# Tile starts at multiples of 128 bytes, the first weight tile loaded in halves, the result stored in runs, and one chunk's order, in a two-layer hybrid encoder trunk

## The chip, the cores and the metric

The kernel runs on one core of a Trainium2 chip. The metric is the device time of one execution in microseconds, lower is better. Before the change it is 2720.67 us (median of three runs).

## The reference, cut to what matters

The input is 512 positions of 1024 channels in float32. Two layers follow each other, each with a half-step feed-forward network, a mixer and a second half-step feed-forward network; a final RMSNorm ends it.

```
for l in range(2):
    x = x + 0.5 * swiglu(rmsnorm(x, ffn1_norm[l]), gate, up, down)        # 1024 -> 2816 -> 1024
    x = x + hybrid_mixer(rmsnorm(x, mix_norm[l]), w_in[l], ...)
    x = x + 0.5 * swiglu(rmsnorm(x, ffn2_norm[l]), gate, up, down)
return rmsnorm(x, final_norm)

def hybrid_mixer(h, ...):
    qkv, g_out, a, b, glu, gates = split(h @ w_in)
    q, k, v = silu(causal_depthwise_conv(qkv, 4 taps))                    # 8 heads of 128
    o = gated_delta_chunked(l2norm(q), l2norm(k), v, g, beta)             # chunked delta rule
    y_a = (rmsnorm(o, head_norm) * silu(g_out)) @ w_a_out
    c = val * sigmoid(gt)
    c = silu(rmsnorm(causal_depthwise_conv(c, 31 taps) + bias, conv_norm))
    y_b = c @ w_b_out
    return (sigmoid(gate_a) * y_a + sigmoid(gate_b) * y_b) @ w_o
```

## The kernel before, in words

**Products.** Everything is held transposed: channels on the 128 partitions, the 512 positions along the free axis. Each float32 operand is split into a high part (`_hi`, type float32r) and the rest (`_lo`), and a product is the sum of three TensorE matmuls, in the order w_hi x act_hi, w_hi x act_lo, w_lo x act_hi (`three`, line 441 on; every matmul is recorded at line 438). The activation is the moving operand and stands first in the names of a row (`h_hi,w_hi`). One output tile of 128 channels from 1024 channels is 8 k-steps of three matmuls, 24 matmuls with 512 columns; a tile of the down projection has 22 k-steps.

**Weights.** Weight tiles of 128x1024 go through four slots: SyncE issues the load into `raw`, ScalarE writes `w_hi` (`hi`, L855), VectorE writes `w_lo` (`lo`, L1235; in the heads a GpSimd DMA does it). TensorE waits for `lo_v`.

**Stages of a layer.** First network: a loop over 11 pairs of gate and up tiles with `h_hi`, `h_lo` as moving operand, then 8 down tiles with `act_hi`, `act_lo`. Mixer: the heads section multiplies `g_hi`, `g_lo` by the tiles of w_in (the first six tiles of a layer still use `h_hi`, `h_lo`), in pieces of 2 to 8 matmuls (mostly 6) between the small 128x128 matmuls of the previous head's delta rule (`PE_ORDER`); two of the gate tiles per chunk for the first three chunks are in it too. Then three tiles of w_a_out on `o_hi`, `o_lo`, three of w_b_out on `c_hi`, `c_lo`, a loop of five rounds with two gate tiles (g), one w_a_out tile (o) and one w_b_out tile (c), and 8 tiles of w_o on `mg_hi`, `mg_lo`. Then the second network. Of the 64 w_in tiles of a layer 6 read h, 48 read g in the heads section and 10 read g in the loop of five.

**Where the tiles lie.** `sb` puts each tile behind the last and rounds every size up to 64 bytes. The first tile, `cst`, lies at byte 16512, which is 129 times 128. The tiles up to `vs` have sizes that are multiples of 128 bytes. `pcol` has 8 x 49 x 4 = 1568 bytes, rounded to 1600, which is 12.5 times 128, so that `ssq`, `sqb`, `hf`, `YD`, `act_hi`, `act_lo`, `g_hi`, `g_lo`, `c_all`, `c_hi`, `mg`, `mg_hi` and `mg_lo` begin 64 bytes past a multiple of 128. `xT`, `h_hi`, `h_lo`, `raw`, `w_hi`, `w_lo`, and `o_hi`, `o_lo` (which share the place of h) begin at a multiple. `q_raw` with 2060 bytes, rounded to 2112, turns this round once more: from `qa` on (`cacc`, `kT`, `XT` and the rest of the delta rule, and `c_lo`) tiles begin at multiples of 128 again.

**The start.** SyncE issues x chunk 0, the first weight tile (512 KB), x chunks 1 to 7, then three more weight tiles. ScalarE issues the identity and then the parameters `pcol`, and multiplies x chunk 0 into `h_hi` when the parameters are there. The first two weight tiles are split by halves (`hi_halves`, `lo_halves`). TensorE runs ten matmuls on `ones` until then.

**The end of the mixer's convolution branch.** For each of 8 chunks VectorE does `c_norm` (L1738), `c_silu` (L1743) and `c_rest` (L1747, writes `c_lo`), ScalarE `c_tanh` (L1184) and the high part `c_hi` (L1191). After the last `c_hi` ScalarE goes on with `hi` of the next weight tiles, and VectorE with `lo`.

**The end.** The last down tile is computed in two halves of 256 positions. For each half: add, square, sum by TensorE, inverse root on GpSimd, spread by TensorE, then `last_norm` on VectorE multiplies in pieces of chunks, in place in `xT`, and SyncE stores each piece.

Of the kernel before, what the change touches and what calls it, by code (L numbers as in the profile page):

```python
# [17 lines left out]
P = 128  # L18
DEPTH, SEQ, D, FF, HEADS = 2, 512, 1024, 2816, 8
KT = D // P  # L20
# [4 lines left out]
EPS = 1e-6  # L25
SLOTS = 4
UNIT = KT * P
DSPLIT = [(0, 8), (8, 16), (16, 22)]
F32, F32R = mybir.dt.float32, mybir.dt.float32r
ACT = mybir.ActivationFunctionType  # L30
# [86 lines left out]
def trunk(nc, x, params_in, ffn1_w_gate, ffn1_w_up, ffn1_w_down, w_in, w_ab, a_log, dt_bias, head_norm, w_a_out, w_b_out, w_o,  # L117
          ffn2_w_gate, ffn2_w_up, ffn2_w_down, consts, out):
    ds = bass.ds
    with ExitStack() as ctx:  # L120
        place = [(nc.sbuf_base + 63) // 64 * 64]

        def sb(name, shape, dt=F32):
            t = nc.alloc_sbuf_tensor_at(name, [P, *shape], dt, offset=place[0])
            place[0] += (4 * int(np.prod(shape)) + 63) // 64 * 64
            return t


# [20 lines left out]
        hnh = sb("hnh", [1])  # L149
        hb = [*hf, *sqb]  # L150
        YD = sb("YD", [2 * P])
        arena = place[0]

        x_sq = sb("x_sq", [KT, SEQ])
# [7 lines left out]


        place[0] = h_at
        o_hi = sb("o_hi", [HEADS, SEQ], F32R)
        o_lo = sb("o_lo", [HEADS, SEQ], F32R)
        place[0] = arena
# [1 line left out]
        g_lo = sb("g_lo", [KT, SEQ], F32R)  # L169
        c_at = place[0]  # L170
        c_all = sb("c_all", [KT, SEQ])
        dn_at = place[0]
        q_raw = sb("q_raw", [SEQ + SC - 1])
        k_raw = sb("k_raw", [SEQ + SC - 1])
# [2 lines left out]
        assert place[0] - dn_at >= 2 * PRE * SEQ * 4  # L177
        c_raw = sb("c_raw", [SEQ + TAPS - 1])
        cacc = [sb(f"cacc{i}", [SEQ]) for i in range(2)]
        delta_at = place[0]  # L180
        (qT, kT, dec, thv, attn, qd, NT, X, XT, Y) = (
            sb(n, [SEQ]) for n in "qT kT dec thv attn qd NT X XT Y".split())
# [4 lines left out]
        hs = sb("hs", [HS_N, NC])  # L187
        sm = sb("sm", [7, NC])
        ksum = sb("ksum", [NC])
        ncol = sb("ncol", [PR_N])  # L190
        dcol = sb("dcol", [PR_N])
        dn_end = place[0]

        place[0] = c_at
# [25 lines left out]
        def sem(name):  # L220
            return ctx.enter_context(nc.semaphore(name))
# [2 lines left out]
        const_in = sem("const_in")  # L224
        ident_in = sem("ident_in")
        x_in = [sem(f"x_in{k}") for k in range(KT)]
        half_hi = sem("half_hi")
        half_lo = sem("half_lo")
        init = sem("init")
# [113 lines left out]
        def _(sp):  # L343
            def x_chunk(k):
                sp.dma_start(xT[:, k, :], x[k]).then_inc(x_in[k], 16)
# [15 lines left out]
            def ffn_units(l, w_gate, w_up, w_down, r_f, v_f, r_d, v_d):  # L361
                first = l == 0 and r_f == R_F1

                def pair_of(i):
                    for c in range(4):
                        src = tile((w_gate, w_up)[c % 2], l, i * 2 + c // 2)
                        unit(l * R_LAYER + i + r_f, l * V_LAYER + i + v_f, lo_v, c, src)
                        if first and isinstance(i, int) and c == 0:
                            for k in range(1, KT):
                                x_chunk(k)  # L370

                if first:
                    pair_of(0)
                with sp.Fori(int(first), FT // 2) as i:
                    pair_of(i)
                if first:
                    sp.dma_start(cst[:, 1:, :], consts[:, 1:, :]).then_inc(const_in, 16)
                if l < DEPTH - 1 and r_f == R_F2:
                    params(l + 1)
                with sp.Fori(0, 2) as i:  # L380
                    for c in range(12):
                        a, b = DSPLIT[c % 3]
                        src = tile(w_down, l, i * 4 + c // 3, a, b)
                        unit(l * R_LAYER + i * 3 + r_d, l * V_LAYER + i * 3 + v_d, lo_v, c, src, b - a)
# [7 lines left out]
            for l in range(DEPTH):  # L392
# [32 lines left out]
                    for c in range(4):  # L425
                        unit(l * R_LAYER + i + R_O, l * V_LAYER + i + V_O, lo_v, c, tile(w_o, l, i * 4 + c))
                ffn_units(l, ffn2_w_gate, ffn2_w_up, ffn2_w_down, R_F2, V_F2, R_D2, V_D2)
            stores = [(0, 0, 4), (0, 4, KT), (1, 0, 3), (1, 3, 6), (1, 6, KT)]
            for h, a, b in stores:
                sp.wait_ge(fin_y, h * KT + b)  # L430
                sp.dma_start(out[a:b].rearrange("k p s -> p k s")[:, :, side(h)], xT[:, a:b, side(h)]).then_inc(stored, 16)
            sp.wait_ge(stored, 16 * len(stores))


# [415 lines left out]
        def _(act):  # L850
# [29 lines left out]
            def ffn(l, w, r_f, r_d, nrm_i, upd0):  # L880
# [23 lines left out]
                for i in range(2):  # L904
                    for c in range(12):
# [22 lines left out]
                        if last and not end:  # L928
                            hi(l * R_LAYER + (r_d + 3 * i), c + 4)

            act.dma_start(cst[:, 0:1, :], consts[:, 0:1, :]).then_inc(ident_in, 16)
            act.dma_start(pcol[:, :, :], params_in[0]).then_inc(par_in, 16)

            def first_x(k):

# [5 lines left out]
                dst = ssq if m == 0 else x_sq[:, m, :]  # L941
                nc.scalar.activation(dst[:, :], xT[:, m, :], ACT.Square).then_inc(sq_done, 1)

            def hi_halves(c):

                act.wait_ge(raw_landed[c], 16)
                act.wait_ge(used, c + 1)
                nc.scalar.activation(w_hi[c][:, 0:UNIT // 2], raw[c][:, 0:UNIT // 2], ACT.Copy).then_inc(half_hi, 1)
                nc.scalar.activation(w_hi[c][:, UNIT // 2:], raw[c][:, UNIT // 2:], ACT.Copy).then_inc(hi_done, 1)

            act.wait_ge(init, 3)
            nc.scalar.activation(nrm[:, 2:4, :], pw[:, :, :], ACT.Copy, scale=pw[:, 1, 0:1])
            act.wait_ge(par_in, 16)
            first_x(0)
            hi_halves(0)
            for k in range(1, KT):
                first_x(k)
            hi_halves(1)
            for m in range(KT):
                square_first(m)  # L960
                if m in (2, 5):
# [267 lines left out]
        def _(dve):  # L1229
# [41 lines left out]
            def ffn(l, w, r_f, v_f, r_d, v_d, nrm_i, nf, row):  # L1271
# [58 lines left out]
                def last_norm(h, a, b):  # L1330

                    dve.wait_ge(fin_bc, h + 1)
                    dve.wait_ge(fin_w, KT - 1 + (h + 1 if b == KT else 0))
                    rs = bank[2 + h][:, side(h)].rearrange("p (k s) -> p k s", k=1).broadcast_to([P, b - a, HALF])
                    tt(xT[:, a:b, side(h)], xT[:, a:b, side(h)], rs, ALU.mult).then_inc(fin_y, b - a)

                for i in range(2):
                    for c in range(12):
                        if end and i == 1 and c == 11:
                            last_add(0)  # L1340
                            last_factor(0)
# [4 lines left out]
                            last_norm(1, 0, 3)  # L1346
# [20 lines left out]
                x_rest(k, PR_F1, 0)  # L1367

            dve.wait_ge(par_in, 16)
            def lo_halves(c):  # L1370

                dve.wait_ge(half_hi, c + 1)
                tt(w_lo[c][:, 0:UNIT // 2], raw[c][:, 0:UNIT // 2], w_hi[c][:, 0:UNIT // 2].bitcast(F32), ALU.subtract).then_inc(half_lo, 1)
                dve.wait_ge(hi_done, c + 1)
                tt(w_lo[c][:, UNIT // 2:], raw[c][:, UNIT // 2:], w_hi[c][:, UNIT // 2:].bitcast(F32), ALU.subtract).then_inc(lo_v, 1)

            first_rest(0)
            lo_halves(0)
            for k in range(1, KT):
                first_rest(k)  # L1380
            lo_halves(1)

            def sum_first(m):

# [9 lines left out]
            for l in range(DEPTH):  # L1394
# [24 lines left out]
                def columns(rd, hd):  # L1419

                    dve.wait_ge(ve_ds.sem, ve_ds.after(rd - 1, "v3"))
                    dve.wait_ge(ac_ds.sem, ac_ds.after(rd - 1, "v_tap"))
                    ts(dcol[:, :], pcol[:, hd, :], 1.0, None, ALU.mult).then_inc(*ve_ds.step("dcol"))
                    dve.wait_ge(ve_ds.sem, ve_ds.after(rd, "dcol"))

                def conv_tap(rd, t, j):
# [92 lines left out]
                def head(dense, hn, rn, before=True):  # L1519
# [41 lines left out]
                    def conv_input():  # L1561

                        if dn:
                            dve.wait_ge(taps, rn * CONV + CONV)
                            ts(ncol[:, :], pcol[:, hn, :], 1.0, None, ALU.mult)
# [196 lines left out]
                c_norm(1)  # L1762
                tail("vE", last)
                for k in range(KT):
                    c_silu(k)
                    if k + 2 < KT:
                        c_norm(k + 2)
                    c_rest(k)
                    if k == 1:
                        tail("oF", last)  # L1770
                        tail("ohi", last, 7)
                        tail("olo", last, 7)
# [189 lines left out]
```

## Time and profile before

| | us |
|---|---|
| runs (3) | 2720.61, 2720.67, 2720.92 |
| median | 2720.67 |
| the profiled execution's own time | 2720.52 |
| its span, first to last instruction | 2718.7 |
| TensorE busy | 2705.3, 100% of the span |
| VectorE busy | 1581.7, 58% |
| ScalarE busy | 1100.1, 40% |
| GpSimd busy | 258.2, 9% |
| mean granted TensorE clock | 0.999 |

Busy times are sums over the span; TensorE's matmuls overlap each other in the records (one is recorded with 390 ns while the next begins 227 ns later), so that the time per matmul is read from the distance of starts and not from the durations.

### The profile page before, as it was taken

What the parts mean: (1) busy time and instruction counts of PE and PEld (TensorE: products, weight loads), DVE (VectorE), ACT (ScalarE), POOL (GpSimd) and SP (SyncE); (2) the same over time, 40 slices, a digit from 0 to 9 for tenths busy, and PEclk for the clock granted to TensorE, in tenths of its full rate; (3) what the DMA queues carried; (4) which work ended last, traced back from release to release, by engine and by line L of the source; (5) the groups of instructions that cost most, each with busy time, mean ns of one, the idle gap of its engine ahead of it and who ended that gap; (6) DMA issues with size and microseconds to landing.
All of it is one profiled execution on the core that took longest, in us unless ns stands there. A gap on an engine that the chain in (4) does not pass through costs nothing.

```text
span 2718.7 us, 35832 instructions
## 1 busy us (share of the span) xinstructions
PE 2705.3 (100%) x13096; PEld 2251.9 (83%) x13096; DVE 1581.7 (58%) x2504; ACT 1100.1 (40%) x1849; POOL 258.2 (9%) x231
## 2 busy tenths in 40 slices
PE   9999999999999999999999999999999999999998
PEld 7888878888887888888888888788888878888887
DVE  6554357888885345553355543688888943455532
ACT  4222247766663232222222222566676622322222
POOL 0000022122120010000000000211212100100000
PEclk9999999999999999999999999999999999999999
DMA  4223335554542222233322233455556332222332
GB/s 166 96 97 104 92 101 140 130 142 111 136 126 93 98 88 100 93 101 93 102 93 93 100 93 96 108 131 140 125 124 145 96 108 93 93 100 93 97 94 66
DMA packets 84603, 292.04 MB, mean 107 GB/s; under 512 B 10001, under 2 KB 12689, under 8 KB 84497
## 3 DMA queue, kind: packets, MB, share of 16 engines
q1 hardware_dynamic: 69232, 235.85, 26.5%
q0 software_dynamic: 14976, 54.53, 10.9%
q8 instruction: 64, 1.05, 0.2%
q14 instruction: 43, 0.34, 0.0%
q10 hardware_dynamic: 288, 0.27, 0.0%
HBM read 233.99 MB, written 2.10 MB: 87 GB/s over the span
## 4 chain that ended last, share of the span: by engine, by line
PE 97%; DVE 2%; ACT 0%; issue 0%; DMA 0%; DVEq 0%; POOLq 0%; POOL 0%; ACTq 0%
PE bank L438 95%; PE bank L637 1%; PE bank L689 1%; DVE c_lo L1747 0%; DVE w_lo L1235 0%; ACT c_hi L1191 0%; PE bank L651 0%; PE bank L725 0%; DVE sqb L1743 0%; DVE hf L1743 0%; DMA pcol<-in_params_in 0%; DVE hf L1738 0%; PE bank L458 0%; DVE NT L1664 0%; ACT w_hi L855 0%
## 5 line engine op out<-in xcount | busy, mean ns | idle before, releaser
L1235 DVE TENSOR_TENSOR w_lo<-raw,w_hi 128x1024 fp32r<-128x1024 f32 x342 | 422.6, 1237 | 542.2 <-ACT w_hi L855 542.1
L855 ACT ACTIVATE w_hi<-raw 128x1024 fp32r<-128x1024 f32 x446 | 469.8, 1055 | 658.7 <-PE bank L438 658.6
L438 PE MATMUL bank<-h_hi,w_hi 128*128 128x512 f32 x1504 | 587.1, 390 | 2.2 <-DVE h_lo L1260 2.1
L438 PE MATMUL bank<-h_hi,w_lo 128*128 128x512 f32 x1504 | 585.5, 389 | 0.0
L438 PE MATMUL bank<-h_lo,w_hi 128*128 128x512 f32 x1504 | 585.3, 389 | 0.0
L438 PE MATMUL bank<-g_hi,w_hi 128*128 128x512 f32 x928 | 384.2, 414 | 0.0
L438 PE MATMUL bank<-g_hi,w_lo 128*128 128x512 f32 x928 | 378.7, 408 | 0.0
L438 PE MATMUL bank<-g_lo,w_hi 128*128 128x512 f32 x928 | 369.6, 398 | 0.0
L438 PEld LDWEIGHTS bank<-h_hi,w_hi 128*128 128x128 f32 x1504 | 282.3, 188 | 63.3 <-issue 3.6
L438 PEld LDWEIGHTS bank<-h_hi,w_lo 128*128 128x128 f32 x1504 | 282.3, 188 | 58.8
L1535 DVE SCALAR_TENSOR_TENSOR cacc<-c_raw,ncol,cacc 128x512 f32<-128x512 f32 x464 | 330.0, 744 | 0.4
L438 PEld LDWEIGHTS bank<-h_lo,w_hi 128*128 128x128 f32 x1504 | 282.4, 188 | 57.7
L438 PE MATMUL bank<-act_hi,w_hi 128*128 128x512 f32 (+1 forms) x726 | 281.3, 387 | 0.0
L438 PE MATMUL bank<-act_hi,w_lo 128*128 128x512 f32 (+1 forms) x726 | 279.6, 385 | 0.0
L438 PE MATMUL bank<-act_lo,w_hi 128*128 128x512 f32 (+1 forms) x726 | 277.0, 382 | 0.0
L890 ACT ACTIVATE hf<-hf 128x512 f32<-128x512 f32 x88 | 55.6, 632 | 447.3 <-DVE hf L1282 447.3
L1845 POOL TENSOR_TENSOR ssq<-ssq,sqb 128x512 f32<-128x512 f32 x41 | 54.8, 1337 | 1708.0 <-ACT sqb L869 1708.0
L438 PEld LDWEIGHTS bank<-g_hi,w_lo 128*128 128x128 f32 x928 | 175.0, 189 | 31.3
L438 PEld LDWEIGHTS bank<-g_lo,w_hi 128*128 128x128 f32 x928 | 175.5, 189 | 28.2
L438 PEld LDWEIGHTS bank<-g_hi,w_hi 128*128 128x128 f32 x928 | 175.9, 190 | 22.9
L438 PEld LDWEIGHTS bank<-act_hi,w_lo 128*128 128x128 f32 x726 | 136.2, 188 | 30.0
L438 PEld LDWEIGHTS bank<-act_lo,w_hi 128*128 128x128 f32 x726 | 136.3, 188 | 28.7
(258 smaller groups left out, 3355.5 us busy)
## 6 DMA issues: line engine op xcount, KB each, us to landing
raw<-in_w_in SPq DMA_DIRECT2D x128, 512.0 KB, 3.3
w_lo<-raw POOLq DMA_DIRECT2D x104, 512.0 KB, 4.6
raw<-in_ffn_w_gate SPq DMA_DIRECT2D x88, 512.0 KB, 3.2
raw<-in_ffn_w_up SPq DMA_DIRECT2D x88, 512.0 KB, 3.2
raw<-in_ffn_w_down SPq DMA_DIRECT2D x64, 512.0 KB, 3.5
raw<-in_ffn_w_down SPq DMA_DIRECT2D x32, 384.0 KB, 3.1
raw<-in_w_a_out SPq DMA_DIRECT2D x16, 512.0 KB, 3.2
raw<-in_w_b_out SPq DMA_DIRECT2D x16, 512.0 KB, 3.2
```

What stands on the lines that cost most here:

```text
L438: return nc.tensor.matmul(o, a, b, start=start, stop=stop, **kw)
L637: m = nc.tensor.transpose(o[:, c * P:c * P + P], a[:, c * P:c * P + P], ident)
L689: m = nc.tensor.transpose(bank[2][:, q * P:q * P + P], X[:, q * P:q * P + P], ident)
L855: nc.scalar.activation(w_hi[c % SLOTS][:, :], raw[c % SLOTS][:, :], ACT.Copy).then_inc(hi_done, 1)
L890: nc.scalar.activation(sg_f[f][:, :], sg_f[f][:, :], ACT.Silu).then_inc(silu_done, 1)
L1235: tt(w_lo[c % SLOTS][:, :], raw[c % SLOTS][:, :], w_hi[c % SLOTS][:, :].bitcast(F32), ALU.subtract).then_inc(lo_v, 1)
L1535: stt(out=acc[:, :], in0=src, scalar=ncol[:, j:j + 1], in1=acc[:, :], op0=ALU.mult, op1=ALU.add).then_inc(taps, 1)
L1845: tt(ssq[:, :], ssq[:, :], sqb[m % 2][:, :], ALU.add).then_inc(sums, 1)
```

## The change

`sb` rounds the place up to a multiple of `LINE` = 128 before a tile of 512 bytes or more, and so do the bases `arena`, `dn_at` and `delta_at`. In the built program every tile of at least 512 bytes then begins at a multiple of 128; those that began at one before keep that property (some move by 256 bytes). The order of tiles is the same.

At the start the first weight tile is loaded by two DMAs of 256 KB with x chunk 1 between them, and ScalarE's and VectorE's work on it is put around x chunk 1 in the same way. ScalarE issues the parameters ahead of the identity. At the end the normed result goes to a tile `y` (at the place of h), which has each half's chunks side by side; the output in memory is laid out as half, partition, chunk, position, and the second half is stored in four pieces (1, 2, 3 and 2 chunks) where it was three (3, 3, 2). The last two chunks of the convolution branch are reordered on VectorE. `ncol` and `dcol` lose one column each, the final norm's, which they didn't use.

```
+LINE = 128
         def sb(name, shape, dt=F32):
+            size = 4 * int(np.prod(shape))
+            if size >= 4 * P:
+                place[0] = (place[0] + LINE - 1) // LINE * LINE
             t = nc.alloc_sbuf_tensor_at(name, [P, *shape], dt, offset=place[0])
-            place[0] += (4 * int(np.prod(shape)) + 63) // 64 * 64
+            place[0] += (size + 63) // 64 * 64
             return t
...
+        place[0] = h_at
+        y = sb("y", [2, KT, HALF])
...
                 if first:
-                    pair_of(0)
+                    halves = raw[0].rearrange("p (h t f) -> p h t f", h=2, t=1)
+                    sp.dma_start(halves[:, 0], tile(w_gate, 0, 0, 0, KT // 2)).then_inc(half_in, 16)
+                    x_chunk(1)
+                    sp.dma_start(halves[:, 1], tile(w_gate, 0, 0, KT // 2, KT)).then_inc(raw_landed[0], 16)
+                    for k in range(2, KT):
+                        x_chunk(k)
+                    for c in range(1, 4):
+                        unit(r_f, v_f, lo_v, c, tile((w_gate, w_up)[c % 2], 0, c // 2))
...
-            stores = [(0, 0, 4), (0, 4, KT), (1, 0, 3), (1, 3, 6), (1, 6, KT)]
+            stores = [(0, 0, 4), (0, 4, KT), (1, 0, 1), (1, 1, 3), (1, 3, 6), (1, 6, KT)]
             for h, a, b in stores:
                 sp.wait_ge(fin_y, h * KT + b)
-                sp.dma_start(out[a:b].rearrange("k p s -> p k s")[:, :, side(h)], xT[:, a:b, side(h)]).then_inc(stored, 16)
+                sp.dma_start(out[h, :, a:b, :], y[:, h, a:b, :]).then_inc(stored, 16)
...
+            act.dma_start(pcol[:, :, :], params_in[0]).then_inc(par_in, 16)
             act.dma_start(cst[:, 0:1, :], consts[:, 0:1, :]).then_inc(ident_in, 16)
-            act.dma_start(pcol[:, :, :], params_in[0]).then_inc(par_in, 16)
...
             first_x(0)
-            hi_halves(0)
-            for k in range(1, KT):
+            hi_half(0, 0)
+            first_x(1)
+            hi_half(0, 1)
+            for k in range(2, KT):
                 first_x(k)
-            hi_halves(1)
+            hi_half(1, 0)
+            hi_half(1, 1)
...
-                    tt(xT[:, a:b, side(h)], xT[:, a:b, side(h)], rs, ALU.mult).then_inc(fin_y, b - a)
+                    tt(y[:, h, a:b, :], xT[:, a:b, side(h)], rs, ALU.mult).then_inc(fin_y, b - a)
...
                 for k in range(KT):
-                    c_silu(k)
+                    if k < KT - 1:
+                        c_silu(k)
                     if k + 2 < KT:
                         c_norm(k + 2)
+                    elif k == KT - 2:
+                        c_silu(KT - 1)
                     c_rest(k)
```

On VectorE at the start, where the residues of x (`h_lo`) and of the first two weight tiles (`w_lo_62`, `w_lo_63`) are made, before:

```order
L1260 SCALAR_TENSOR_TENSOR h_lo<-xT,pcol,h_hi 128x512
L1373 TENSOR_TENSOR w_lo_62<-raw_54,w_hi_58 128x512
L1375 TENSOR_TENSOR w_lo_62<-raw_54,w_hi_58 128x512
L1260 SCALAR_TENSOR_TENSOR h_lo<-xT,pcol,h_hi 128x512 x7
L1373 TENSOR_TENSOR w_lo_63<-raw_55,w_hi_59 128x512
L1375 TENSOR_TENSOR w_lo_63<-raw_55,w_hi_59 128x512
```

and of the change:

```order
L1277 SCALAR_TENSOR_TENSOR h_lo<-xT,pcol,h_hi 128x512
L1392 TENSOR_TENSOR w_lo_62<-raw_54,w_hi_58 128x512
L1277 SCALAR_TENSOR_TENSOR h_lo<-xT,pcol,h_hi 128x512
L1392 TENSOR_TENSOR w_lo_62<-raw_54,w_hi_58 128x512
L1277 SCALAR_TENSOR_TENSOR h_lo<-xT,pcol,h_hi 128x512 x6
L1392 TENSOR_TENSOR w_lo_63<-raw_55,w_hi_59 128x512 x2
```

The second x chunk's residue moved ahead of the second half of the first weight tile; nothing behind the third chunk moved.

On VectorE at the end of the convolution branch in layer 0, where `cth` is the tanh, `c_lo` the residue of a chunk and `w_lo_64` the next weight tile's, before:

```order
811 L1743 SCALAR_TENSOR_TENSOR sqb_70<-cth_124,sqb_70 128x512
812 L1747 TENSOR_TENSOR c_lo<-sqb_70,c_hi 128x512
813 L1743 SCALAR_TENSOR_TENSOR sqb_71<-cth_125,sqb_71 128x512
814 L1747 TENSOR_TENSOR c_lo<-sqb_71,c_hi 128x512
815 L1235 TENSOR_TENSOR w_lo_64<-raw_56,w_hi_60 128x1024
```

and of the change:

```order
811 L1763 SCALAR_TENSOR_TENSOR sqb_70<-cth_125,sqb_70 128x512
812 L1763 SCALAR_TENSOR_TENSOR sqb_71<-cth_126,sqb_71 128x512
813 L1767 TENSOR_TENSOR c_lo<-sqb_70,c_hi 128x512
814 L1767 TENSOR_TENSOR c_lo<-sqb_71,c_hi 128x512
815 L1252 TENSOR_TENSOR w_lo_64<-raw_56,w_hi_60 128x1024
```

The last chunk's product (on `sqb_71`) moved ahead of the residue of the chunk before it.

## Rows read from the trace of the kernel before

**Rows 1.** The page, busy time of each engine.

```profile
PE 2705.3 (100%) x13096; PEld 2251.9 (83%) x13096; DVE 1581.7 (58%) x2504; ACT 1100.1 (40%) x1849; POOL 258.2 (9%) x231
```

**Rows 2.** Waits of TensorE: who for whom, us in total, times, longest.

```profile
PE bank L438 <- DVE w_lo L1235: 1.0, 2, 0.5
...
PE bank L438 <- DVE c_lo L1747: 0.5, 2, 0.2
```

**Rows 3.** Timeline of TensorE, gate and up tiles: start, duration, engine, what.

```profile
200.52 0.39 PE L438 MATMUL bank<-h_hi,w_hi 128*128 128x512 f32 x1
...
203.92 0.39 PE L438 MATMUL bank<-h_hi,w_hi 128*128 128x512 f32 x1
```

**Rows 4.** Timeline of TensorE, down tiles.

```profile
340.13 0.39 PE L438 MATMUL bank<-act_hi,w_hi 128*128 128x512 f32 x1
...
343.57 0.39 PE L438 MATMUL bank<-act_hi,w_hi 128*128 128x512 f32 x1
```

**Rows 5.** Timeline of TensorE, loop of five rounds and w_o: tiles' first matmuls.

```profile
930.13 0.40 PE L438 MATMUL bank<-g_hi,w_hi 128*128 128x512 f32 x1
...
941.13 0.40 PE L438 MATMUL bank<-o_hi,w_hi 128*128 128x512 f32 x1
...
943.22 0.39 PE L438 MATMUL bank<-o_hi,w_hi 128*128 128x512 f32 x1
...
946.62 0.40 PE L438 MATMUL bank<-c_hi,w_hi 128*128 128x512 f32 x1
...
952.20 0.40 PE L438 MATMUL bank<-mg_hi,w_hi 128*128 128x512 f32 x1
...
996.16 0.40 PE L438 MATMUL bank<-h_hi,w_hi 128*128 128x512 f32 x1
```

**Rows 6.** Timeline of TensorE: six matmuls after small ones, three places.

```profile
375.29 0.48 PE L438 MATMUL bank<-h_hi,w_hi 128*128 128x512 f32 x1
...
376.74 0.39 PE L438 MATMUL bank<-h_hi,w_hi 128*128 128x512 f32 x1
...
525.18 0.48 PE L438 MATMUL bank<-g_hi,w_hi 128*128 128x512 f32 x1
...
526.65 0.38 PE L689 MATMUL bank<-cst,X 128*128 128x128 f32 x2
...
814.96 0.48 PE L438 MATMUL bank<-o_hi,w_hi 128*128 128x512 f32 x1
...
816.44 0.39 PE L438 MATMUL bank<-o_hi,w_hi 128*128 128x512 f32 x1
```

**Rows 7.** Timeline, end of the convolution branch, layer 0; idle time before in brackets.

```profile
829.20 0.50 PE L438 MATMUL bank<-c_hi,w_hi 128*128 128x512 f32 x1 [0.23 <-DVE c_lo L1747]
...
830.68 0.50 PE L438 MATMUL bank<-c_hi,w_hi 128*128 128x512 f32 x1 [0.52 <-DVE w_lo L1235]
...
828.45 0.69 DVE L1747 TENSOR_TENSOR c_lo<-sqb,c_hi 128x512 fp32r<-128x512 f32 x1 [0.70 <-ACT c_hi L1191]
829.40 1.23 DVE L1235 TENSOR_TENSOR w_lo<-raw,w_hi 128x1024 fp32r<-128x1024 f32 x1 [0.26 <-ACT w_hi L855]
```

**Rows 8.** Timeline, the start (DMA issues with the queue's name).

```profile
1.18 0.45 ACTq L932 DMA_DIRECT2D pcol<-in_params_in  x1
...
5.71 0.72 ACT L878 ACTIVATE h_hi<-xT,pcol 128x512 fp32r<-128x512 f32 x1 [2.45 <-DMA pcol<-in_params_in]
...
7.38 4.39 ACT L878 ACTIVATE h_hi<-xT,pcol 128x512 fp32r<-128x512 f32 x7
...
9.25 0.50 PE L438 MATMUL bank<-h_hi,w_hi 128*128 128x512 f32 x1 [0.18 <-DVE h_lo L1260]
...
11.90 0.63 ACT L948 ACTIVATE w_hi<-raw 128x512 fp32r<-128x512 f32 x1
...
14.19 0.39 PE L438 MATMUL bank<-h_hi,w_hi 128*128 128x512 f32 x1
```

**Rows 9.** The end: VectorE's last norms, and DMA share and GB/s of one stretch.

```profile
2712.82 2.41 DVE L1335 TENSOR_TENSOR xT<-xT,bank 128x768 f32<-128x768 f32 x3 [1.36 <-PE bank L530]
...
2715.50:2716.00 0.50, 0.00 (x0) 0.00 (x0) 0.00 (x0) 0.00 (x0) 0.00 (x0) 0.50 1.04 352
```

More of the change, by code:

```diff
@@ L120, in trunk @@
     with ExitStack() as ctx:
-        place = [(nc.sbuf_base + 63) // 64 * 64]
+        place = [(nc.sbuf_base + LINE - 1) // LINE * LINE]
         def sb(name, shape, dt=F32):
+            size = 4 * int(np.prod(shape))
+            if size >= 4 * P:
+                place[0] = (place[0] + LINE - 1) // LINE * LINE
             t = nc.alloc_sbuf_tensor_at(name, [P, *shape], dt, offset=place[0])
-            place[0] += (4 * int(np.prod(shape)) + 63) // 64 * 64
+            place[0] += (size + 63) // 64 * 64
             return t
@@ L151, in trunk @@
         YD = sb("YD", [2 * P])
+        place[0] = (place[0] + LINE - 1) // LINE * LINE
         arena = place[0]
@@ L171, in trunk @@
         c_all = sb("c_all", [KT, SEQ])
+        place[0] = (place[0] + LINE - 1) // LINE * LINE
         dn_at = place[0]
@@ L179, in trunk @@
         cacc = [sb(f"cacc{i}", [SEQ]) for i in range(2)]
+        place[0] = (place[0] + LINE - 1) // LINE * LINE
         delta_at = place[0]
@@ L189, in trunk @@
         ksum = sb("ksum", [NC])
-        ncol = sb("ncol", [PR_N])
-        dcol = sb("dcol", [PR_N])
+        ncol = sb("ncol", [PR_FIN])
+        dcol = sb("dcol", [PR_FIN])
         dn_end = place[0]
@@ L226, in trunk @@
         x_in = [sem(f"x_in{k}") for k in range(KT)]
+        half_in = sem("half_in")
         half_hi = sem("half_hi")
@@ L367, in pair_of @@
                         unit(l * R_LAYER + i + r_f, l * V_LAYER + i + v_f, lo_v, c, src)
-                        if first and isinstance(i, int) and c == 0:
-                            for k in range(1, KT):
-                                x_chunk(k)
                 if first:
-                    pair_of(0)
+                    halves = raw[0].rearrange("p (h t f) -> p h t f", h=2, t=1)
[6 more added lines that the diff above has]
+                        unit(r_f, v_f, lo_v, c, tile((w_gate, w_up)[c % 2], 0, c // 2))
                 with sp.Fori(int(first), FT // 2) as i:
@@ L942, in square_first, with hi_half @@
                 nc.scalar.activation(dst[:, :], xT[:, m, :], ACT.Square).then_inc(sq_done, 1)
-            def hi_halves(c):
-                act.wait_ge(raw_landed[c], 16)
+            def hi_half(c, h):
+                t = slice(h * (UNIT // 2), (h + 1) * (UNIT // 2))
+                act.wait_ge(half_in if c + h == 0 else raw_landed[c], 16)
                 act.wait_ge(used, c + 1)
-                nc.scalar.activation(w_hi[c][:, 0:UNIT // 2], raw[c][:, 0:UNIT // 2], ACT.Copy).then_inc(half_hi, 1)
-                nc.scalar.activation(w_hi[c][:, UNIT // 2:], raw[c][:, UNIT // 2:], ACT.Copy).then_inc(hi_done, 1)
+                nc.scalar.activation(w_hi[c][:, t], raw[c][:, t], ACT.Copy).then_inc((half_hi, hi_done)[h], 1)
             act.wait_ge(init, 3)
@@ L954, in _ @@
             first_x(0)
-            hi_halves(0)
-            for k in range(1, KT):
+            hi_half(0, 0)
+            first_x(1)
+            hi_half(0, 1)
+            for k in range(2, KT):
                 first_x(k)
-            hi_halves(1)
+            hi_half(1, 0)
+            hi_half(1, 1)
             for m in range(KT):
@@ L1345, in ffn @@
                             last_factor(1)
-                            last_norm(1, 0, 3)
+                            last_norm(1, 0, 1)
+                            last_norm(1, 1, 3)
                             last_norm(1, 3, 6)
@@ L1369, in _, with lo_half @@
             dve.wait_ge(par_in, 16)
[L1370 to L1375, printed above, removed]
+            def lo_half(c, h):
+                t = slice(h * (UNIT // 2), (h + 1) * (UNIT // 2))
+                dve.wait_ge((half_hi, hi_done)[h], c + 1)
+                tt(w_lo[c][:, t], raw[c][:, t], w_hi[c][:, t].bitcast(F32), ALU.subtract).then_inc((half_lo, lo_v)[h], 1)
             first_rest(0)
-            lo_halves(0)
-            for k in range(1, KT):
+            lo_half(0, 0)
+            first_rest(1)
+            lo_half(0, 1)
+            for k in range(2, KT):
                 first_rest(k)
-            lo_halves(1)
+            lo_half(1, 0)
+            lo_half(1, 1)
             def sum_first(m):
@@ L1422, in columns @@
                     dve.wait_ge(ac_ds.sem, ac_ds.after(rd - 1, "v_tap"))
-                    ts(dcol[:, :], pcol[:, hd, :], 1.0, None, ALU.mult).then_inc(*ve_ds.step("dcol"))
+                    ts(dcol[:, :], pcol[:, hd, 0:PR_FIN], 1.0, None, ALU.mult).then_inc(*ve_ds.step("dcol"))
                     dve.wait_ge(ve_ds.sem, ve_ds.after(rd, "dcol"))
@@ L1564, in conv_input @@
                             dve.wait_ge(taps, rn * CONV + CONV)
-                            ts(ncol[:, :], pcol[:, hn, :], 1.0, None, ALU.mult)
+                            ts(ncol[:, :], pcol[:, hn, 0:PR_FIN], 1.0, None, ALU.mult)
                             dve.wait_ge(ac_ds.sem, ac_ds.after(rn, "gt_th"))
@@ L1957 @@
         args.append(nc.dram_tensor(f"in_{name}", a.shape, mybir.dt.from_np(a.dtype), kind="ExternalInput").ap())
-    out = nc.dram_tensor("out_x", (KT, P, SEQ), F32, kind="ExternalOutput").ap()
+    out = nc.dram_tensor("out_x", (2, P, KT, HALF), F32, kind="ExternalOutput").ap()
     trunk(nc, *args, out)
     y = _run(nc, [arrays], core_ids=[0]).results[0]["out_x"]
-    return np.ascontiguousarray(y.reshape(D, SEQ).T)[None]
+    return np.ascontiguousarray(y.transpose(0, 3, 2, 1).reshape(SEQ, D))[None]
```

## The prediction

> **What bounds the kernel now.** I began with the busy times: TensorE is busy for 2705.3 of 2718.7 us [rows 1]. The waits of TensorE come next: those on VectorE at line 1235 and on `c_lo` add up to 1.5 us, twice per kernel each [rows 2], and the rest is the start and the end. So time can be won in two ways only: each matmul takes less, or one of the few gaps closes. The third view is the timeline of TensorE, read as the distance between starts. It shows that equal matmuls (512 columns, same weights' shape, no wait) don't cost the same in every stage:
>
> - gate and up tiles, operand h: from 200.52 to 203.92 are 15 matmuls, 3.40 us, 680 ns for the three of a k-step [rows 3];
> - down tiles, operand act: 340.13 to 343.57, 15 matmuls, 3.44 us, 688 ns for three [rows 4];
> - g in the loop of five rounds: 930.13 to 941.13, two tiles, 5.50 us each, 687.5 ns for three; o: 5.49 us the tile, but its last five k-steps, 943.22 to 946.62, are 3.40 us, again 680 ns; c: 946.62 to 952.20, 5.58 us, 697.5 ns for three; mg: 952.20 to 996.16, eight tiles, 43.96 us, 687 ns for three [rows 5].
>
> By the addresses of the section on the kernel, h and o begin at a multiple of 128 bytes; act, g, c_hi and mg begin 64 bytes off, and c_lo at a multiple. The two that lie even settle at 680 ns, though o stands in the same loop as g and c, with the same work on the other engines. The two engines beside it don't explain it, and the offset does. A tile of 24 matmuls at the even rate is 8 x 0.680 = 5.44 us.
>
> **Alignment, in the loops.** It adds no instruction. For the down tiles: 4 networks x 8 tiles x 22 k-steps are 704; the difference is 7 ns (one row pair says 8 at a resolution of 10 ns, mg's long stretch, off by the same 64 bytes, says 7; I take 6.7), which makes 4.7 us. For g, 2 layers x 10 tiles x (5.50 - 5.44) = 1.2 us. For o, 10 tiles x 0.05 = 0.5 us: its first three k-steps are slow behind a g tile, and would not be when g is even. For c, 16 tiles x (5.58 - 5.44) = 2.2 us. For mg, 16 tiles x 0.055 = 0.9 us. Together 9.5 us, all of it on TensorE and so on the path. Bounds: 0 if the offset isn't the cause, 10.5 with act at 8 ns.
>
> **Alignment, in the heads.** Here 48 tiles of each layer read g, but in pieces of mostly six matmuls between small ones. Six matmuls from 525.18 to 526.65 take 1.47 us [rows 6]. The even tiles show after a break 1.45 us (375.29 to 376.74, h) and 1.48 us (814.96 to 816.44, o) [rows 6]. The first matmul behind a break takes some 0.32 us whatever it reads, and the next ones are slow on even tiles too, as the first k-steps of o are. So the pieces gain between -0.01 and 0.02 us. There are 2 x 48 x 4 = 384 pieces' worth: from about -4 to 8 us. The likelier end is near zero, since most breaks in the heads are transposes and 128x128 products as before 814.96; I take 4 ns each, 1.5 us.
>
> The Trainium skill's page "SBUF — State Buffer" (section "Specifications (TRN2)") gives SBUF lines of 16 bytes, with a penalty for each access that crosses to a new line. An offset of 64 bytes is even by that, and the alignment would give nothing; the rows of 680 beside 687 ns speak against it. With it the sum would be the one of the first rival below.
>
> **The convolution branch.** Before, the last chunk's `c_lo` started at 828.45, having waited 0.70 us for ScalarE, and the next weight tile's `w_lo` at 829.40 [rows 7]. TensorE waited for both: its matmul at 829.20 idled 0.23 us by the row, and that at 830.68 idled 0.52 us [rows 7]. Counted against a steady stream this is more: from 829.20 to 830.68 are three matmuls, 1.48 us where they take 0.70, so 0.78 us for the second gap with the slow first matmul, and about 0.5 us for the first. That is 1.28 us per layer. With the product of the last chunk done while ScalarE works on the one before it, both that product (0.6 us) and the wait of 0.70 us go from between the last two residues. ScalarE's last `c_hi` begins when the product ends, so it and the next `w_hi` come 1.3 us earlier too, and `w_lo` starts at 828.1 instead of 829.40. TensorE could use it 1.28 us after its start (829.40 to 830.68), so now at 829.38. Without gaps TensorE wants that tile at 830.68 - 1.28 = 829.40, or 0.1 earlier if c tiles run at the even rate. Nothing is late next by more than that 0.1 us. Two layers: 2.5 us; bounds 2.0 and 2.6. No wait is added: the product that is moved needs a tanh that was done long before.
>
> **The start.** The parameters were issued at 1.18, behind the identity, and `h_hi` of chunk 0 waited for them until 5.71 [rows 8]. They now go first and share the engines with one x chunk instead of with 512 KB of weights behind it, so they land at least 0.4 us earlier, perhaps 1.7. TensorE's second k-step waited for VectorE until 9.25 [rows 8]; its residue is now one 0.6 us instruction earlier. But the gain ends at the second weight tile. ScalarE finished the x chunks at 7.38 + 4.39 = 11.77 and started the second tile's half at 11.90, a gap of 0.13 us that only the landing explains [rows 8]. As many bytes as before stand ahead of it, so it lands at 11.9 again. From there 0.6 for `w_hi`, 0.7 for `w_lo` and the semaphores give TensorE the tile at about 13.35; it began it at 14.19 [rows 8]. So 0.8 us, bounds 0.3 and 1.3. The identity, now second, is wanted only after the warming matmuls. The one DMA more on SyncE delays the later loads' issue by 0.45 us, under the queue of bytes that hides it.
>
> **The end.** The first piece of the last half is one chunk instead of three, so and the norms take 2.41 us for eight chunks, 0.3 us a chunk [rows 9], so that its store starts 0.6 us earlier; one instruction more makes the last norm end 0.1 us later (it was 2712.82 + 2.41 = 2715.23). The stores run at 352 GB/s with the DMA engines full [rows 9], so 1 MB takes 3.0 us, and the last piece still queues behind the others. Replaying the pieces at that rate gives 0.3 us; if longer runs move faster, 0.6. I take 0.4, bounds 0 and 0.7. The cut of one column in `ncol` and `dcol` is nothing: VectorE has idle time in the heads.
>
> **The sum** is 9.5 + 1.5 + 2.5 + 0.8 + 0.4 = 14.7 us. The profiled execution took 2720.52 us (span 2718.7 and 1.8 around it), 0.15 below the median. 2720.67 - 14.7 = 2706.0 us.
>
> **Rivals.**
> 1. The offset isn't the cause (it may be the place in SBUF: h and o share one address, all the slow ones lie higher). Then only the three small edits count, 3.7 us: 2717.0. For it: c_lo lies even and high, and the c tiles are the slowest of all. Against it: mg, act and g differ in place and agree within 1 ns.
> 2. Slower: the odd one out is a sign. If what is slow about c is the even-and-high tile against weights at their present place, every operand moved to such a place takes c's rate, 697.5 instead of 687 ns per three. It decides on 704 k-steps of act, 160 of g and 128 of mg: 992 x 10.5 ns = 10.4 us lost, less the 3.7, 2727.4. The one row for it is c's; against it, the matmuls of c alternate between even and off tiles, which after the change none does.
> 3. The heads gain too: pieces come down to the 1.45 us of h. 384 x 0.023 = 8.8 instead of 1.5 us: 2698.7. For it: after the sums at 375 the even tile shows it; against: o at 815 doesn't.
> 4. The alignment works on act, g and mg alone and c keeps a slow rate, or the reverse: 7 to 9 us off in all, about 2712.
> 5. The layout doesn't come out even. The sizes say it does, so this is left at next to nothing.
>
> **How the numbers follow.** Forecast 0.52, rival 1 0.18, rival 2 0.07, rival 3 0.13, rival 4 0.10. The range from 2698 to 2717.5 takes in the first, third and fourth and most of rival 1, and leaves the slower case and the far ends out. A difference of 0.2% is 5.4 us, about what can be told from no change; rival 1 falls inside it. Faster 0.75, within 0.2% 0.18, slower 0.07.
>
> **What would show it.** In the profile after, 15 matmuls of the down tiles in 3.40 us; c, g and mg tiles at 5.44 us each; six matmuls in the heads still at 1.47 us; no wait of TensorE on `c_lo` or `w_lo` in the convolution branch; the second weight tile's first matmul near 13.4; the last store done 0.4 us sooner after the last norm's start. It is wrong if act stays at 687 ns per three, or if the pieces of six in the heads come out at 1.45 us.

## The result, and the profile after

| | before | changed |
|---|---|---|
| runs | 5, median 2720.79 us (2720.61 to 2720.93) | 5, median 2732.88 us (2732.52 to 2733.16) |
| profiled execution, span | 2720.52, 2718.7 | 2732.52, 2730.7 |
| TensorE busy | 2705.3 | 2720.1 |

The ratio is 1.0044 (95% interval 1.0031 to 1.0057): the changed kernel is slower by 12.1 us, where 14.7 us less were forecast. The granted clock is 0.999 in both profiles, and the number of matmuls is the same. The busy times of the changed kernel answer to [rows 1]:

```profile
PE 2720.1 (100%) x13096; PEld 2253.9 (83%) x13096; DVE 1583.1 (58%) x2505; ACT 1100.7 (40%) x1849; POOL 257.7 (9%) x231
```

TensorE is the path as before, and its waits are short. The view of waits (engine, line, for whom, us in total, times, longest) answers to [rows 2]. The waits for `c_lo` and for `w_lo` of L1235 are gone, as forecast; nothing else became late:

```profile
PE bank L452 <- ACT sqb L931: 1.2, 1, 1.2
PE bank L452 <- DVE pw L1381: 1.1, 1, 1.1
PE bank L544 <- POOL nrm L1940: 1.0, 1, 1.0
PE bank L452 <- DVE XT L1689: 0.5, 2, 0.3
PE bank L452 <- issue: 0.4, 1, 0.4
PE bank L452 <- DVE h_lo L1277: 0.4, 1, 0.4
```

So the 12 us lie in the matmuls themselves. Timeline of TensorE after, with the starts as in [rows 3 to 6]: gate and up tiles, down tiles, a piece of six in the heads, and the loop of five rounds with w_o behind it:

```profile
199.64 0.39 PE L452 MATMUL bank<-h_hi,w_hi 128*128 128x512 f32 x1
...
203.04 0.39 PE L452 MATMUL bank<-h_hi,w_hi 128*128 128x512 f32 x1
...
340.27 0.40 PE L452 MATMUL bank<-act_hi,w_hi 128*128 128x512 f32 x1
...
343.78 0.39 PE L452 MATMUL bank<-act_hi,w_hi 128*128 128x512 f32 x1
...
523.71 0.48 PE L452 MATMUL bank<-g_hi,w_hi 128*128 128x512 f32 x1
...
525.20 0.38 PE L703 MATMUL bank<-cst,X 128*128 128x128 f32 x2
...
932.85 0.40 PE L452 MATMUL bank<-g_hi,w_hi 128*128 128x512 f32 x1
...
944.05 0.39 PE L452 MATMUL bank<-o_hi,w_hi 128*128 128x512 f32 x1
...
949.50 0.40 PE L452 MATMUL bank<-c_hi,w_hi 128*128 128x512 f32 x1
...
955.09 0.40 PE L452 MATMUL bank<-mg_hi,w_hi 128*128 128x512 f32 x1
...
999.89 0.39 PE L452 MATMUL bank<-h_hi,w_hi 128*128 128x512 f32 x1
```

Fifteen matmuls on h still take 3.40 us. Fifteen on act take 3.51 where [rows 4] has 3.44. Two g tiles take 11.20 us (11.00 in [rows 5]), the o tile 5.45 (5.49), the c tile 5.59 (5.58), eight mg tiles 44.80 (43.96). Averaged over whole stages (in layer 0 the 528 matmuls on act of one network, the 240 on g in the loop of five and the 192 on mg), the three matmuls of a k-step take 700 ns in act, g and mg, where they took 687. The budget of the difference:

| term | count x ns | us |
|---|---|---|
| act | 704 k-steps x 13.2 | +9.3 |
| g in the loop of five | 160 x 12.3 | +2.0 |
| mg | 128 x 13.2 | +1.7 |
| o, c | 10 tiles x -40, 16 x 10 | -0.2 |
| g in the heads | 384 pieces x 5.8 (254 pieces of six matmuls: mean 1478.9 after, 1473.1 before) | +2.2 |
| start, convolution branch, end | see the second experiment | -2.8 |
| sum | | +12.2 |

Measured are 12.1.

### The profile page after: what moved, and what is told of

Same layout as the page of the kernel before. It is cut to its first block, busy times and chain, and to the rows that moved or that the text cites. A ratio compares the mean times of both kernels' runs of the same rounds, so it can differ in the third digit from the quotient of the medians.

```text
span 2730.7 us, 35838 instructions
## 1 busy us (share of the span) xinstructions
PE 2720.1 (100%) x13096; PEld 2253.9 (83%) x13096; DVE 1583.1 (58%) x2505; ACT 1100.7 (40%) x1849; POOL 257.7 (9%) x231
## 4 chain that ended last, share of the span: by engine, by line
PE 99%; DVE 0%; issue 0%; DMA 0%; DVEq 0%; POOLq 0%; ACT 0%; POOL 0%
PE bank L452 97%; PE bank L651 1%; PE bank L703 1%; PE bank L665 0%; PE bank L739 0%; DMA pcol<-in_params_in 0%; PE bank L472 0%; DVE NT L1684 0%; DVE h_lo L1277 0%; DVE XT L1689 0%; DVE y L1352 0%; DVE w_lo L1392 0%; PE bank L815 0%; DVEq L121 0%; POOLq L121 0%
## 5 line engine op out<-in xcount | busy, mean ns | idle before, releaser
L452 PEld LDWEIGHTS bank<-act_hi,w_hi 128*128 128x128 f32 x726 | 136.4, 188 | 31.1
```

Source lines behind the costliest of these rows:

```text
L452: return nc.tensor.matmul(o, a, b, start=start, stop=stop, **kw)
```

## The experiments

The question was why tiles that were moved to a multiple of 128 became slower while h, which lies at one, is the fastest. Listing the addresses of the built programs modulo 256 gave the theory. "Distance" below is the address of the moving operand minus that of the weights, modulo 256. The weights (`w_hi`, `w_lo`) begin at 128 modulo 256 in both kernels, and both steps from one k-step to the next (512 bytes in the weights, 2048 in the moving tile) keep the distance.

| tile | distance before | ns per three | distance after | ns per three |
|---|---|---|---|---|
| h | 0 | 681 | 0 | 681 |
| act, g, mg | 64 | 687 | 128 | 700 |
| c_hi / c_lo | 64 / 128 | 697 | 128 / 128 | 699 |
| o | 0 | 685, first k-steps slower | 0 | 682 |

**1. The alignment alone.** Before, with `LINE` and the roundings (and `ncol`, `dcol` one column shorter, as in the change):

```
+            if size >= 4 * P:
+                place[0] = (place[0] + LINE - 1) // LINE * LINE
```

> The alignment alone, without the other edits. From the two traces (down tiles 687 to 700 ns per three, w_o 687 to 700, loop of five and heads slower): about 15 us slower than before, 2736 us. If the other edits are what costs, it is the same as before.

2735.6 us, ratio 1.0055 (1.0038 to 1.0072). The profile has 700.0 ns per three on act. The alignment by itself costs 15 us.

**2. The edits alone.** The change with `LINE = 64`, so that no tile moves:

```
-LINE = 128
+LINE = 64
```

> The change with its alignment turned off (LINE = 64, the place of every tile as before): the start, the end and the order of the last chunk alone. By the two traces 0.4 us at the start, 2.6 us in the convolution branch and 0 to 0.4 us at the end: 2717.5 us. If the edits cost, above 2720.8.

2717.83 us, ratio 0.999 (0.998 to 1.0), 2.8 us below the kernel before in the same job (2720.65); the interval touches 1, but no run of the one reaches the fast runs of the other (2717.65 to 2718.38 and 2720.37 to 2721.16). The two parts add up: +15.0 and -2.8. Act is back at 686.8.

**3. Matmuls with nothing beside them.** Before, with 26 stretches of 48 matmuls of 512 columns appended at the end, all other engines idle; the text of the expectation counts one stretch too many. The first two stretches only warm up. Operands are views of act, h and the weight tiles begun at other bytes:

```
+for n_, (reg, rh, rl, wo) in enumerate(...):   # region, bytes of hi, of lo, of the weights
+    mm(bank[4][:, :], wt[0][:, w], f[:, k * SEQ + e:k * SEQ + e + SEQ], start=j == 0, stop=j == 2)
```

> The kernel before, with a series of extra matmuls on TensorE behind its last work, when the other engines have nothing left but the last norms and stores: 27 stretches of 48 matmuls (128x512, the order w_hi x hi, w_hi x lo, w_lo x hi), each with the moving operand or the weights begun at another byte. The stretches' results are not used; the kernel's own output is the full one. Numbers are the address modulo 512 of moving hi, moving lo and weights. Theory R (relation): the rate depends on the moving operand's place against the weights' place modulo 256, 680 ns per three matmuls when equal, 687 at 64 bytes apart, 700 at 128 apart. Then moving 128 and 384 with weights at 128 give 680, 0 and 256 give 700, the others 687; moving 128 with weights at 256 gives 700; moving 256 with weights at 256 gives 680. Theory A (absolute): only the moving operand's own place counts, so moving 128 gives 680 whatever the weights' place is, and moving 256 gives 700 with weights at 256 too. Theory S (region in SBUF): the place of act gives slow rates at every offset and the place of h fast ones at every offset. Theory C (contention with the work of ScalarE, VectorE and DMA on the weights): with those engines idle all stretches take the same, 680.

Timeline of TensorE in the stretches of distance 0, 128 and 64 (the first two rows, the next two, the last two), 15 matmuls from one row to the other of a pair:

```profile
2728.34 0.39 PE L438 MATMUL bank<-act_hi,w_hi 128*128 128x512 f32 x1
...
2731.74 0.39 PE L438 MATMUL bank<-act_hi,w_hi 128*128 128x512 f32 x1
...
2740.92 0.40 PE L438 MATMUL bank<-act_hi,w_hi 128*128 128x512 f32 x1
...
2744.41 0.39 PE L438 MATMUL bank<-act_hi,w_hi 128*128 128x512 f32 x1
...
2773.43 0.39 PE L438 MATMUL bank<-act_hi,w_hi 128*128 128x512 f32 x1
...
2776.86 0.39 PE L438 MATMUL bank<-act_hi,w_hi 128*128 128x512 f32 x1
```

These are 3.40, 3.49 and 3.43 us. The same operand of the same tile is fast or slow by where it begins. Over the last 33 matmuls of a stretch, in ns per three: distance 0 680, 64 687, 128 697 to 700, 192 700. The first k-steps of a stretch are slower (778, 690, 697 and 684 ns in one of distance 0). The distances 0, 64 and 128 came out alike in the act region and in the h region. All four came out alike when the weights were moved and the moving operand stayed (moving at 128 modulo 512: weights at 192, 256, 320, 384 gave 700, 700, 687, 680). Both at a multiple of 256 gave 680, and so did both at 128. So neither the absolute alignment nor the region nor work of other engines makes the steps of 7 to 20 ns; the distance modulo 256 does. The absolute place is worth 3 ns at most here: at distance 128 a moving operand at a multiple of 512 took 697, one at 256 modulo 512 took 700, in both regions. Where hi and lo differ no rule of mine holds: hi at distance 0 with lo at 128 gave 700, hi at 128 with lo at 0 gave 687.

**4. All the slow tiles at distance 0, by a pad.** Before, with 192 free bytes ahead of `arena`, where act, g, c and mg begin (and `ncol`, `dcol` one column shorter, as in the change):

```
+        place[0] += 192
```

> The kernel before with nothing but 192 bytes left free ahead of the arena (and the two copies of parameters one column shorter, so that it fits): act, g, c_hi, mg_hi, mg_lo then begin at 128 modulo 512, as h and the weights do; c_lo begins at 448. Theories R and A: the down tiles fall from 687 to 680 ns per three, mg and g in the loop of five too, the c tiles don't reach 680 because c_lo is off; 4.7 + 1.2 + 0.9 + 0.5 us less, some 2713 us, and less by up to 5 us more if the heads gain. Theory S: the down tiles stay at 687 or above and the time is 2720 or more.

2712.58 us, ratio 0.997 (0.9959 to 0.9982), 8 us less for a line that computes nothing. The forecast was some 2713. Act, g and mg take 680.0 to 681.2 ns per three. Only c stays slow, 695, since its `c_lo` lies 64 from the weights and `c_hi` 0.

**5. The counterproof: h moved away.** The kernel of 4, with the weight slots ahead of `xT` and 128 bytes between, so that h and o get distance 128 and every other tile keeps its distance:

```
+        raw = ...; w_hi = ...; w_lo = ...       # ahead of xT
+        place[0] += 128
...
-        place[0] += 192
+        place[0] += 64
```

> The run with 192 bytes of padding (2712.6 us), with one thing more: raw, w_hi and w_lo are placed ahead of xT, and 128 bytes stand between, so that h and o lie 128 bytes (modulo 256) from the weights, and act, g, c_hi, mg as before in that run at a multiple of 256 from them. The order of instructions is the same. Theory R: the gate and up tiles on h, 4 x 22 tiles x 8 k-steps x 2 layers' share (1504 k-steps with the first six tiles of each mixer), go from 680 to 699 ns per three: 28 us more, o in the loop of five 2 more, near 2742. Rival (h and o are fast because of where they lie in SBUF, not by the distance to the weights): unchanged within 2 us of 2712.6.

2741.29 us, ratio 1.0075 (1.006 to 1.0091). Gate and up tiles in its timeline:

```profile
200.23 0.39 PE L440 MATMUL bank<-h_hi,w_hi 128*128 128x512 f32 x1
...
203.71 0.39 PE L440 MATMUL bank<-h_hi,w_hi 128*128 128x512 f32 x1
```

3.48 us where h had 3.40 in every kernel so far. The time is 28.7 us above that of 4; 30 were expected.

**6. Everything at distance 0, with the three edits.** The change, with another rule of placing:

```
-LINE = 128
+LINE, AT = 256, 128
-                place[0] = (place[0] + LINE - 1) // LINE * LINE
+                place[0] = (place[0] - AT + LINE - 1) // LINE * LINE + AT
```

(`q_raw`, `k_raw`, `v_raw` are left out, and `hf`, `ncol`, `dcol` change places in the order, so that all fits.)

> The changed kernel with one other rule of placing: tiles of 512 bytes and more begin 128 bytes past a multiple of 256, which is where the weight tiles w_hi and w_lo lie, instead of at multiples of 128. So act, g, c_hi, c_lo, mg, h and o all lie at a multiple of 256 bytes from the weights. The three edits of the order (start, end, convolution branch) are kept. Theory R (the time of a matmul goes by the distance of moving operand and weights modulo 256: 0 gives 680 ns per three, 64 gives 687, 128 gives 699): act, g in the loop of five, o, mg and c all at 680 per three; against the kernel before act 704 x 6.9 = 4.8 us, g 1.2, mg 0.9, o 0.5, c 2.2 less, the edits 2.8, the heads 0 to 5: 2703 to 2708 us, most likely 2707.8. If it is the multiple of 128 itself that hurts: slower than before, near 2733. If the edits hurt: about 2711.

2707.48 us, ratio 0.9951 (0.9937 to 0.9964): faster than both kernels, within 0.3 us of the expectation. Its page and its loop:

```profile
PE 2695.5 (100%) x13096; PEld 2252.2 (83%) x13096; DVE 1582.7 (58%) x2505; ACT 1099.7 (41%) x1849; POOL 257.7 (10%) x231
```

```profile
340.25 0.39 PE L452 MATMUL bank<-act_hi,w_hi 128*128 128x512 f32 x1
...
343.65 0.39 PE L452 MATMUL bank<-act_hi,w_hi 128*128 128x512 f32 x1
...
925.22 0.39 PE L452 MATMUL bank<-g_hi,w_hi 128*128 128x512 f32 x1
...
936.10 0.39 PE L452 MATMUL bank<-o_hi,w_hi 128*128 128x512 f32 x1
...
941.54 0.39 PE L452 MATMUL bank<-c_hi,w_hi 128*128 128x512 f32 x1
...
946.98 0.39 PE L452 MATMUL bank<-mg_hi,w_hi 128*128 128x512 f32 x1
...
990.50 0.39 PE L452 MATMUL bank<-h_hi,w_hi 128*128 128x512 f32 x1
```

Act 3.40 us, every tile of the loop 5.44, mg 43.52 / 8 = 5.44. That is the profile that was forecast for the change, under another condition.

**7. The steps between, and short pieces.** Before, with stretches appended as in 3: distances in steps of 16 bytes, matmuls of 256 columns, and pieces of six, each with four 128x128 transposes behind it. In these pieces the weights stay in place; what the expectation calls the weights' offset is, in the run, the place of the transposed operand:

```
+for d in (0, 16, 32, 48, 80, 96, 112, 144, 160, 176, 208, 224, 240):
+    mark()
+    series(d, 48)
```

> The kernel before with stretches of matmuls appended, no other engine at work; only the time per three is of interest. First two warm stretches, then stretches of 48 matmuls of 512 columns with the moving operand d bytes (modulo 256) past the weights, d = 0, 16, 32, 48, 80, 96, 112, 144, 160, 176, 208, 224, 240; then matmuls of 256 columns with d = 0, 64, 128, 192 (96 each); then eight pieces of six matmuls behind four 128x128 transposes, with all pairs of the weights' offset and d among 0, 64, 128, 192. Theory R: between the known points 680 (d=0 and 192 when the moving operand is 64 below), 687 (64), 699 (128) the steps of 16 bytes lie at or above the neighbours' times, none below 680, which is the floor. If a finer period is at work, some of them fall below 680. In the pieces: d = 128 costs 4 matmuls per piece some 19/3 ns each, so 0.02 to 0.04 us a piece more than d = 0; if breaks hide it, no difference. The length of a piece at d = 0 is 1.47 us.

The values are good to about 1 ns:

| distance | ns per three | distance | ns per three |
|---|---|---|---|
| 0 | 680.0 | 128 (from 3) | 697 to 700 |
| 16 | 695.5 | 144 | 700.0 |
| 32 | 700.0 | 160 | 703.6 |
| 48 | 700.0 | 176 | 700.0 |
| 64 (from 3) | 687 | 192 (from 3) | 700 |
| 80 | 693.6 | 208 | 704.5 |
| 96 | 700.0 | 224 | 700.0 |
| 112 | 693.6 | 240 | 710.0 |

Nothing falls below 680, so distance 0 is the best of the sixteen. The expectation that a step lies at or above both neighbours held for most; 80 and 112 lie between 64 and 128. In the pieces of six I expected 20 to 40 ns more at 128 than at 0. With the transposed operand at its own place, eight pieces with their transposes take 14.83 us at distance 0, 14.88 at 128 and 14.93 at 192: 6 and 12 ns a piece. In pieces most of the effect is hidden, and the place of the transposed operand is worth as much: with it 64 bytes further, distances 0 and 128 both take 14.88. The 256-column matmuls don't follow the rule. Behind the first k-step of a stretch three take 360 ns at distance 0, 353 at 64, 356 at 128 and 340 at 192. They occur only in the last tile here, and why they differ is open.

**8. The end.** Counted from the start of VectorE's last norms, the last stores of the changed kernel end earlier, but its span doesn't. These norms start at 2712.82 before [rows 9] and in the changed kernel here:

```profile
2724.77 2.48 DVE L1352 TENSOR_TENSOR y<-xT,bank 128x256 f32<-128x256 f32 x4 [1.30 <-PE bank L544]
```

The rows of the closing line (a row: line, queue, operation, count, ns, start) of the changed kernel:

```profile
L121 POOLq EVENT_SEMAPHORE  x2: 17/17/17, 2730.5 to 2730.6; - x2
...
L121 POOLq DRAIN  x1: 6985/6985/6985, 2723.5 to 2723.5; - x1
...
L121 SPq DRAIN  x1: 7/7/7, 2730.0 to 2730.0; - x1
L121 SPq EVENT_SEMAPHORE  x1: 17/17/17, 2730.7 to 2730.7; - x1
```

and of before:

```profile
L120 POOLq DRAIN  x1: 6985/6985/6985, 2711.5 to 2711.5; - x1
...
L120 SPq DRAIN  x1: 7/7/7, 2718.5 to 2718.5; - x1
```

GpSimd's drain starts with its last instruction, the inverse root, and lasts 6.985 us in both. Before, it ended at 2718.5, when the stores were done too. After, SyncE is done at 2730.0 and GpSimd at 2730.5. The test takes the last inverse root away from the kernel of 6 (the last 256 positions are then scaled by a wrong factor):

```
-            for h in range(2):
+            for h in range(1):
                 pool.wait_ge(fin_var, h + 1)
```

> The kernel of e5_same with the inverse root of the last half left out: GpSimd's last instruction is then the first half's inverse root, and VectorE writes the mean square itself as the factor (so the last 256 positions are scaled by a wrong factor). Two theories on why the four stores of the changed end gained nothing. Theory G: in every profile so far GpSimd's closing drain lasts 6.985 us and starts when its last instruction does, so that the span cannot end before the last inverse root plus 7.1 us, while the stores of the change are done 0.5 us before that. Without the last inverse root the span ends 5.4 us after the last norms' start instead of 6.0 (e5_same), and the drain of GpSimd ends far earlier. Theory N: the end goes by the stores and something behind them, and stays at 6.0 us after the last norms' start. In both the norms start about 0.75 us sooner, since the instruction and its semaphores are gone: 2706.1 us by G, 2706.7 by N.

2706.54 us, ratio 0.9948 (0.9931 to 0.9965). VectorE's last norms and the closing line:

```profile
2699.28 2.48 DVE L1355 TENSOR_TENSOR y<-xT,bank 128x256 f32<-128x256 f32 x4 [0.53 <-PE bank L544]
```

```profile
L121 POOLq DRAIN  x1: 6995/6995/6995, 2691.7 to 2691.7; - x1
...
L121 SPq DRAIN  x1: 7/7/7, 2704.5 to 2704.5; - x1
```

The span ends at 2704.7, 5.42 us behind the norms' start, where the kernel of 6 took 5.96 (2699.61 to 2705.56). That is theory G. The time by itself doesn't tell the two theories apart: 2706.54 lies 0.4 us above G's number and 0.2 below N's. In this profile the last addition stood 0.45 us later than in that of 6 (2697.03 and 2696.58), which the stages ahead made and which accounts for G's 0.4. A correct kernel without the late root on GpSimd wasn't tried, so whether these 0.5 us can be had is open.

## Why the prediction was wrong

**Alignment, in the loops (forecast -9.5, measured about +12.8).** The reading of the rows was right: equal matmuls cost 680, 687 or 697 ns per three by the tile they read. The step that failed is "The two engines beside it don't explain it, and the offset does", with the offset taken against multiples of 128 and of the moving tile alone. What counts is the moving operand's distance from the weights modulo 256. Of the two tiles that lay "even", h and o also lay at distance 0, and four that lay off lay at distance 64; a multiple of 128 and distance 0 could not be told apart by these six. The seventh could: `c_lo` lay at a multiple of 128, at distance 128, in the slowest tile. The prediction wrote this down as support for its first rival and set it aside, and that was the row to follow. With the true cause the same sum stands: in experiment 6 the loops took 680 everywhere, and the 9.5 us, the edits' 2.8 and the heads' 1.5 add up to 13.8 where 13.5 were measured.

**Rival 2** had the sign, the place and the mechanism's outline: tiles moved to an even place take c's rate. It gave 2727.4 and got a chance of 0.07. What it missed are 2.5 ns per three (700 instead of 697.5, 992 k-steps, 2.5 us), the heads (2.2 us) and 0.9 us less from the edits (2.8 instead of 3.7). That is 5.6, and 5.5 were missing. Its argument against itself, that c alternates between even and off tiles, was no reason: with both at distance 128 c takes 699.

**Heads (forecast -1.5, measured +2.2).** The pieces of six went from 1.473 to 1.479 us. At distance 0 (experiment 6) they take 1.469, 4 ns less, the number that was forecast. Rival 3 (23 ns a piece) has nothing for it.

**Convolution branch (forecast -2.5).** Right. VectorE in layer 0 after, which answers to [rows 7], makes both products and then both residues, and `w_lo` follows:

```profile
828.31 1.29 DVE L1763 SCALAR_TENSOR_TENSOR sqb<-cth,sqb 128x512 f32<-128x512 f32 x2
...
829.03 1.24 ACT L1208 ACTIVATE c_hi<-sqb 128x512 fp32r<-128x512 f32 x2 [0.70 <-DVE sqb L1763]
...
829.69 1.30 DVE L1767 TENSOR_TENSOR c_lo<-sqb,c_hi 128x512 fp32r<-128x512 f32 x2
...
831.25 1.23 DVE L1252 TENSOR_TENSOR w_lo<-raw,w_hi 128x1024 fp32r<-128x1024 f32 x1 [0.26 <-ACT w_hi L869]
```

TensorE has no gap there. From the first matmul of the mixer to the loop of five, the kernel of experiment 2 takes 1.27 us less than before in layer 0 and 1.31 in layer 1, 2.6 of the edits' 2.8.

**Start (forecast -0.8, measured next to nothing).** The parameters came 0.8 us sooner, as forecast. The second weight tile didn't land at 11.9. The rows answer to [rows 8]:

```profile
4.92 0.72 ACT L892 ACTIVATE h_hi<-xT,pcol 128x512 fp32r<-128x512 f32 x1 [1.64 <-DMA pcol<-in_params_in]
...
6.04 0.43 SPq L369 DMA_DIRECT2D raw<-in_ffn_w_up  x1
...
12.36 1.15 ACT L963 ACTIVATE w_hi<-raw 128x512 fp32r<-128x512 f32 x2 [0.56 <-DMA raw<-in_ffn_w_up]
...
13.78 0.50 PE L452 MATMUL bank<-h_hi,w_hi 128*128 128x512 f32 x1
```

SyncE issued it at 6.04; before it was 5.18, with one DMA less ahead of it. ScalarE waited for its landing until 12.36, and TensorE began it at 13.78 instead of 14.19. The k-step behind this wait was a slow one, and at the tile's fifth k-step TensorE was 0.24 us ahead of before (16.67 against 16.91). The same k-step stands at 16.51, 16.93 and 16.94 in the three other profiles with the new start, and at 16.68 to 16.99 in four more with the old one, so that nothing clear of their scatter was won. The step that failed is "As many bytes as before stand ahead of it, so it lands at 11.9 again". The bytes are the same, but fewer of them had moved: by 7.0 us the DMA engines had moved 1.57 to 1.63 MB in the four profiles with the new start, and 1.74 to 1.82 in the six with the old. At the rate of the x chunks behind (0.26 MB in 0.67 us), 0.2 MB are 0.5 us. The later issue isn't what cost them: x chunk 2 already lands at 7.70 instead of 7.19, and the weight tile lands 1.28 us behind the last x chunk in both. Which of the edits slows the first 7 us, the halves or the parameters going first, was not tried.

**End (forecast -0.4, measured 0).** The stores are done 0.4 us sooner after the norms' start (SyncE's drain at +5.2 instead of +5.6), which is the forecast. The step that failed is the silent one, that the last store ends the kernel. GpSimd's drain ended with it before, and ends 0.5 us behind it after (experiment 8).

## What to carry to other kernels

When equal matmuls take unequal times by the tile they read, list the addresses of both operands, moving and weights, and compare their difference modulo 256, not each one's alignment; here a pad of 192 bytes gave 8 us and the rounding to 128 lost 15. Before a chance is given to a rule with one exception in the profile, the exception has to be explained by it. At an end of a program, look at every engine's drain, since the last store need not be what the end waits for.

## What the hardware showed that I had not expected

- With float32r operands of 128x512 and weights of 128x128 the pitch of matmuls goes by the distance of moving operand and weights modulo 256 bytes: 226.7 ns each at 0, 229 at 64, 232 to 233 at 128, 233 at 192, up to 238 at a distance of 4 bytes (713 ns per three, a stretch of experiment 3). It is the same with all other engines idle. Which part of the chip makes it was not found, nor why hi and lo at distances 0 and 128 give 700 one way round and 687 the other.
- At 256 columns distance 192 is the fast one (340 ns per three against 360 at 0).
- GpSimd's closing drain takes 6.98 to 7.00 us from the start of its last instruction in all ten profiles, and in the changed kernel it ends later than the last store.
